# Expert blocks of a routed MoE: the next block's rows transposed behind the gate and up products, and loaded as half rows on 128 partitions

## The reference, cut to what matters

```
A = T * TOP_K_IN_GROUP                      # 512 tokens, 2 experts each
...                                         # assignments sorted by expert, rows padded to blocks
def run_block(args):
    tok, e, wt = args
    xb = h[tok]
    y = (jax.nn.silu(xb @ w_g[e]) * (xb @ w_u[e])) @ w_d[e]
    return y.astype(jnp.float32) * wt[:, None]
...
out = jnp.zeros((T, D), jnp.float32).at[row_tok].add(ys.reshape(P, D))
```

## Time and profile before

| | us |
|---|---|
| median of 3 runs (3201.56 to 3216.19) | 3206.61 |
| the profiled execution, its own time | 3209.52 |
| its span, first to last instruction | 3207.7 |

### The profile page before, as it was taken

How to read it: one execution, slowest core, us unless ns; L and a number is a source line. 1 busy time by engine, 2 the same in 40 slices (tenths; PEclk the granted TensorE clock), 3 DMA queues, 4 the chain that set the end, 5 groups by cost and what they waited for, 6 DMA issues and landing times.

```text
span 3207.7 us, 29346 instructions
## 1 busy us (share of the span) xinstructions
PE 2334.1 (73%) x9978; PEld 1037.1 (32%) x9978; DVE 1449.1 (45%) x3427; ACT 730.4 (23%) x1764; POOL 616.6 (19%) x604
## 2 busy tenths in 40 slices
PE   2998999966777778489976797655775665665554
PEld 1444554442333333145555644221221111111110
DVE  1395520140000000210127766755767777777775
ACT  2005420011000000121225544222222322232222
POOL 1001100000000000100001222234444444444442
PEclk8999999968998898788888878777878877788776
DMA  7417824818999999542105676789999999999996
GB/s 265 154 53 241 299 72 133 260 73 322 387 378 379 371 377 387 177 142 94 53 27 209 267 306 242 298 331 393 416 418 421 422 421 421 421 409 421 421 421 271
DMA packets 207405, 928.24 MB, mean 289 GB/s; under 512 B 18857, under 2 KB 58856, under 8 KB 124846
## 3 DMA queue, kind: packets, MB, share of 16 engines
q0 software_dynamic: 80752, 558.26, 43.0%
q1 hardware_dynamic: 116736, 359.68, 30.9%
q10 hardware_dynamic: 9790, 8.73, 0.8%
HBM read 891.42 MB, written 35.18 MB: 289 GB/s over the span
## 4 chain that ended last, share of the span: by engine, by line
PE 30%; DMA 25%; DVE 11%; ACT 5%; issue 5%; POOL 1%; ACTq 1%; DVEq 0%; SPq 0%; POOLq 0%
DMA ring<-in_expert_pair,ids 13%; PE bank L2026 7%; PE bank L1820 7%; DMA ring<-in_w_exp_up 6%; PE bank L2333 4%; DVE ring L1769 4%; PE bank L1826 3%; DMA pair_last<-in_expert_pair,ids 2%; PE bank L2039 2%; DMA arena_v<-in_expert_pair,ids 2%; DMA arena_h<-in_expert_pair,ids 2%; ACT arena_w L1222 1%; PE bank L2346 1%; POOL ring L845 1%; DVE pair_last L1769 1%
## 5 line engine op out<-in xcount | busy, mean ns | idle before, releaser
L2333 PE MATMUL bank<-ring,arena_w 128*32 128x512 f32 x1568 | 550.9, 821 | 359.9 <-ACT arena_w L1222 359.8
L845 POOL DMA_INDIRECT ring<-in_expert_pair,ids x392 | 424.8, 1084 | 1125.9 <-PE bank L2333 674.4
L1820 PE MATMUL bank<-arena_h,ring 128*128 128x512 f32 (+1 forms) x1024 | 372.2, 524 | 12.8 <-DMA ring<-in_w_in 10.7
L2026 PE MATMUL bank<-ring,arena_h 128*64 128x512 f32 x1056 | 288.8, 707 | 78.1 <-DMA ring<-in_w_exp_up 39.1
L2333 PEld LDWEIGHTS bank<-ring,arena_w 128*32 128x32 f32 x1568 | 94.6, 131 | 673.6 <-ACT arena_w L1222 506.7
L1769 DVE CUSTOM_DVE_ANT_0 ring<-ring,arena_h 128x1024 f32<-128x1024 f32 x203 | 245.8, 1226 | 123.1 <-DMA ring<-in_expert_pair,ids 90.0
L1769 DVE CUSTOM_DVE_ANT_0 ring<-ring 128x1024 f32<-128x1024 f32 x189 | 229.6, 1225 | 77.3 <-DMA ring<-in_expert_pair,ids 69.0
L1515 DVE TENSOR_TENSOR arena_q<-arena_q,bank 128x256 f32<-128x256 f32 x32 | 13.5, 421 | 536.9 <-ACT arena_q L1006 536.9
L1820 PEld LDWEIGHTS bank<-arena_h,ring 128*128 128x128 f32 x1024 | 178.6, 196 | 195.6 <-issue 192.6
L1220 ACT ACTIVATE arena_w<-arena_w 128x2 f32<-128x2 f32 (+1 forms) x224 | 45.6, 203 | 763.7 <-DVE arena_w L1769 763.4
L2026 PEld LDWEIGHTS bank<-ring,arena_h 128*64 128x64 f32 x1056 | 107.3, 162 | 235.0 <-issue 202.3
(11 more groups left out here) (465 smaller groups left out, 3199.4 us busy)
## 6 DMA issues: line engine op xcount, KB each, us to landing
ring<-in_w_exp_gate SPq DMA_DIRECT2D x33, 2048.0 KB, 20.2
ring<-in_w_exp_up SPq DMA_DIRECT2D x33, 2048.0 KB, 24.9
ring<-in_w_exp_down SPq DMA_DIRECT2D x33, 2048.0 KB, 25.4
ring<-in_w_in SPq DMA_DIRECT2D x15, 2048.0 KB, 22.3
ring<-in_w_mod SPq DMA_DIRECT2D x12, 2048.0 KB, 11.9
ring<-in_w_ada SPq DMA_DIRECT2D x12, 2048.0 KB, 17.7
xs_d<-zeros SPq DMA_DIRECT2D x1, 12032.0 KB, 69.3
arena_h<-xs_d SPq DMA_DIRECT2D x33, 256.0 KB, 25.6
```

The lines of the kernel that those rows point to most:

```text
L845: pool.indirect_dma_start(pair[pair_of(m)], None, A["expert_pair_2"], bass.IndirectOffsetOnAxis(ap=ids[n % 2][:, r:r + 1], axis=0)).then_i ...
L1820: mm = pe.matmul(dst, w[:, c, at], rhs[:, c, :], start=(c == 0), stop=(c == chunks - 1))
L2026: mm = pe.matmul(bank[2 + b][at, :].rearrange("p (g f) -> p g f", g=2), xbT[b][:, c, :], gu[:, :, c, 256 * half:256 * half + 256], start=( ...
L2333: mm = pe.matmul(bank[4 + 2 * (n // H % 2) + half][at, :], sel_q[:, n % 2, k0 + j, :], pair[pair_of(m + j)][:, D + 512 * half:D + 512 * ha ...
```

## The change

The rows are loaded as two half rows of 2 KB, values 0 to 511 on partitions 0 to 63 and values 512 to 1023 on partitions 64 to 127; so four transposes of 128x128 take the place of eight of 64x128. For the chunks of `xbT` to fit, partition p now takes the gate and up rows 4p to 4p+3 and 512+4p to 512+4p+3: two pieces of 8 KB. In the streams of TensorE and ScalarE the work is put in another order: transposes of e+1 between gate/up of e and down of e; the copy of e+1 ahead of e's result. The overflow block has the new layout and keeps its order.

```diff
-        xblk = [arena_h[0:CAP, D * i:D * i + D] for i in range(2)]
+        xblk = [arena_h[:, 512 * i:512 * i + 512] for i in range(2)]
...
-            return w[e, :, :].rearrange("(p c) n -> p c n", c=DC)
+            return w[e, :, :].rearrange("(h p c) n -> p h c n", h=2, c=DC // 2)
...
             def rows(e, b):
                 unless_first(sp, xbT_done, e - 1)
-                sp.dma_start(xblk[b], xs_d[bass.ds(e * CAP, CAP), :]).then_inc(xb_in[b], 16)
+                for half in range(2):
+                    sp.dma_start(xblk[b][CAP * half:CAP * half + CAP, :], xs_d[bass.ds(e * CAP, CAP), 512 * half:512 * half + 512])\
+                        .then_inc(xb_in[b], 16)
...
-                        sp.dma_start(slab(n + k), A[w][bass.ds(e, 1), :, :].rearrange("o (p c) n -> p (o c) n", c=DC))\
+                        sp.dma_start(slab2h(n + k), A[w][bass.ds(e, 1), :, :].rearrange("o (h p c) n -> p (o h) c n", h=2, c=DC // 2))\
...
-            def expert(e, b, i):
+            def columns_in(e, b):
                 act.wait_ge(xbT_done, e + 1)
                 unless_first(act, gu_done, e - 1)
-                act.activation(xbT[b], bank[b][:, :].rearrange("p (a c) -> p a c", c=CAP), ACT.Copy).then_inc(xbT_out, 1)
+                act.activation(xbT[b].rearrange("p (h c) t -> p h c t", h=2), bank[b][:, :].rearrange("p (c h t) -> p h c t", h=2, t=CAP),
+                               ACT.Copy).then_inc(xbT_out, 1)
+
+            def gate(e, b):
                 act.wait_ge(gu_done, e + 1)
...
+            def rows_out(e, b, i):
                 act.wait_ge(dn_done, e + 1)
...
+            def two(i):
+                columns_in(i * 2, 0)
+                rows_out(i * 2 - 1, 1, i - 1)
+                gate(i * 2, 0)
+                columns_in(i * 2 + 1, 1)
+                rows_out(i * 2, 0, i)
+                gate(i * 2 + 1, 1)
...
             def block_T(b):
-                for c in range(DC):
-                    mm = pe.transpose(bank[b][:, c * CAP:(c + 1) * CAP], xblk[b][:, c:D:DC], ident[0:CAP, 0:CAP])
+                for c in range(DC // 2):
+                    mm = pe.transpose(bank[b][:, c * P:(c + 1) * P], xblk[b][:, c:512:DC // 2], ident[:, :])
...
+            def columns(b, i):
+                pe.wait_ge(xb_in[b], i * 32 + 32)
+                pe.sem_inc(mark, 1)
+                block_T(b).then_inc(xbT_done, 1)
+
+            def gate_up(e, b, i):
                 pe.wait_ge(xbT_out, e + 1)
...
+            def down(e, b, i):
                 pe.wait_ge(hid_done, e + 1)
                 hidden_T(b).then_inc(hidT_pe, 1)
                 pe.wait_ge(hidT_done, e + 1)
-                arrived(2)
-                unless_first(pe, yv_done, e - 1)
-                block_dn(b, n + 2).then_inc(dn_done, 1)
+                arrived(b, i, 2)
+                unless_first(pe, yv_done, e)
+                block_dn(b, N_EXP + 3 * b + 2).then_inc(dn_done, 1)
...
+            columns(0, 0)
+            gate_up(0, 0, 0)
+            columns(1, 0)
+            down(0, 0, 0)
+            gate_up(1, 1, 0)
             with pe.Fori(1, NE // 2) as i:
-                for b in range(2):
-                    expert(i * 2 + b, b, i)
+                columns(0, i)
+                down(i * 2 - 1, 1, i - 1)
+                gate_up(i * 2, 0, i)
+                columns(1, i)
+                down(i * 2, 0, i)
+                gate_up(i * 2 + 1, 1, i)
+            down(NE - 1, 1, NE // 2 - 1)
```

More of the change, by code:

```diff
@@ L491, in build @@
         for e in range(2):
-            slabs += [(w_gu(A["w_exp_gate"], e), (DC, F), gu_done, 2 * NE), (w_gu(A["w_exp_up"], e), (DC, F), gu_done, 2 * NE),
+            slabs += [(w_gu(A["w_exp_gate"], e), (2, DC // 2, F), gu_done, 2 * NE), (w_gu(A["w_exp_up"], e), (2, DC // 2, F), gu_done, 2 * NE),
                       (w_dn(A["w_exp_down"], e), (2, 2, D), dn_done, 2 * NE)]
@@ L662, in _ @@
                     e = sp.value_load(over_i[0:1, bass.ds(i + 1, 1)], min_val=0, max_val=NE - 1)
-                    sp.dma_start(xblk[0], xs_d[bass.ds(i * CAP + NE * CAP, CAP), :]).then_inc(ov_xin, 16)
+                    for half in range(2):
+                        sp.dma_start(xblk[0][CAP * half:CAP * half + CAP, :],
+                                     xs_d[bass.ds(i * CAP + NE * CAP, CAP), 512 * half:512 * half + 512]).then_inc(ov_xin, 16)
                     for w, k in (("w_exp_gate", 0), ("w_exp_up", 1)):
-                        sp.dma_start(slab(N_EXP + k), A[w][bass.ds(e, 1), :, :].rearrange("o (p c) n -> p (o c) n", c=DC))\
+                        sp.dma_start(slab2h(N_EXP + k), A[w][bass.ds(e, 1), :, :].rearrange("o (h p c) n -> p (o h) c n", h=2, c=DC // 2))\
                             .then_inc(ov_slab, 16)
@@ L1013, in expert @@
                                   yblk[b][CAP * half:CAP * half + CAP, :]).then_inc(y_dma[b], 16)
-            for b in range(2):
-                expert(b, b, 0)
-            with act.Fori(1, NE // 2) as i:
-                for b in range(2):
-                    expert(i * 2 + b, b, i)
+            columns_in(0, 0)
+            gate(0, 0)
+            columns_in(1, 1)
+            rows_out(0, 0, 0)
+            gate(1, 1)
+            def two(i):
[5 more added lines that the diff above has]
+                gate(i * 2 + 1, 1)
+            two(1)
+            with act.Fori(2, NE // 2) as i:
+                two(i)
+            rows_out(NE - 1, 1, NE // 2 - 1)
             act.wait_ge(route_done, 2)
@@ L1024, in _ @@
                     act.wait_ge(xbT_done, i + (NE + 1))
-                    act.activation(xbT[0], bank[0][:, :].rearrange("p (a c) -> p a c", c=CAP), ACT.Copy).then_inc(xbT_out, 1)
+                    act.activation(xbT[0].rearrange("p (h c) t -> p h c t", h=2), bank[0][:, :].rearrange("p (c h t) -> p h c t", h=2, t=CAP),
+                                   ACT.Copy).then_inc(xbT_out, 1)
                     act.wait_ge(gu_done, i + (NE + 1))
@@ L2041, in block_dn, with arrived @@
                 return mm
-            def expert(e, b, i):
-                n = N_EXP + 3 * b
-                def arrived(k):
-                    pe.wait_ge(slab_in[(n + k) % RING], i * 16 + 16 * ((n + k) // RING + 1))
-                pe.wait_ge(xb_in[b], i * 16 + 16)
+            def arrived(b, i, k):
+                n = N_EXP + 3 * b + k
+                pe.wait_ge(slab_in[n % RING], i * 16 + 16 * (n // RING + 1))
+            def columns(b, i):
+                pe.wait_ge(xb_in[b], i * 32 + 32)
                 pe.sem_inc(mark, 1)
                 block_T(b).then_inc(xbT_done, 1)
+            def gate_up(e, b, i):
                 pe.wait_ge(xbT_out, e + 1)
-                arrived(0)
-                arrived(1)
-                block_gu(b, n).then_inc(gu_done, 1)
+                arrived(b, i, 0)
+                arrived(b, i, 1)
+                block_gu(b, N_EXP + 3 * b).then_inc(gu_done, 1)
+            def down(e, b, i):
                 pe.wait_ge(hid_done, e + 1)
@@ L2058, in expert @@
                 pe.wait_ge(hidT_done, e + 1)
-                arrived(2)
-                unless_first(pe, yv_done, e - 1)
-                block_dn(b, n + 2).then_inc(dn_done, 1)
+                arrived(b, i, 2)
+                unless_first(pe, yv_done, e)
+                block_dn(b, N_EXP + 3 * b + 2).then_inc(dn_done, 1)
             pe.wait_ge(route_done, 2)
             pe.wait_ge(skT_done, 5)
-            for b in range(2):
-                expert(b, b, 0)
-            with pe.Fori(1, NE // 2) as i:
-                for b in range(2):
-                    expert(i * 2 + b, b, i)
+            columns(0, 0)
[3 more added lines that the diff above has]
+            gate_up(1, 1, 0)
+            with pe.Fori(1, NE // 2) as i:
+                columns(0, i)
[5 more added lines that the diff above has]
+            down(NE - 1, 1, NE // 2 - 1)
             n_over = pe.value_load(over_i[0:1, 0:1], min_val=0, max_val=OVER)
@@ L2072, in _ @@
                 with pe.If(i < n_over):
-                    pe.wait_ge(ov_xin, i * 16 + 16)
+                    pe.wait_ge(ov_xin, i * 32 + 32)
                     pe.sem_inc(mark, 1)
```

2 lines of the change are left out of this document (added).

## The result

The changed kernel takes 3181.48 us, median of 5 runs (3168.23 to 3188.50), against 3212.97 for the kernel before, run beside it 5 times: ratio 0.990, 95% interval 0.9879 to 0.992. That is 32 us or 1.0%, twice what can be told from no change. The forecast's own narrower range, 3190 to 3215, missed it; that the wide one holds it is because it was drawn to make room for the first rival (3171), so it is luck for the mechanism that was forecast.

A forecast was written before the change was run, and what follows sets the result against it. The prediction took the slabs' DMA rate, 18.26 us a block, as the bound. Terms -3.4 + 0.9 + 3 + 1.4 (rows in 2 KB pieces) - 3.7 = -1.8 us, on the median 3206.6 about 3205; range 3168 to 3222.

The forecast's parts named there:

- the first rival: Row loads: 64-partition rows hold up other transfers' writes; an even spread gives back 33 us, about 3171; chance 0.22.
- the one on the bound: Expert blocks: slabs at 18.26 us a block are the bound; TensorE's own period of 17.6 us is shorter.
- the pieces rival: Two lagging DMA engines: more pieces cost 50 ns each, +1.0 us a block, +30, giving 3234; chance 0.16.
- the rows rival: The same as the first rival; its sign was a rate over 395 GB/s in slices 10 to 15.
- The order: TensorE and ScalarE streams: saves TensorE 2.8 us a block, which turns into waiting for up slabs; gains only at the end.
- The gain at the end, -3.4: Expert 31: gate/up starts when its up slab lands, not 3.4 us after: -3.4 us.
- The clock's +0.9: Expert 31's gate/up: slower after a longer wait, between 0 and +1.3 us, taken as +0.9.
- Rows on 128 partitions: Row loads: the 64-partition form costs 0.5 us a block; a quarter comes back, -3.7 us, range 0 to -15.
- the damage to neighbours of the outermost bound: Expert-block DMA: 2.2 us a block unassigned to any transfer, possibly harm to neighbouring transfers; -66 us as outermost end.
- Pieces: Gate and up slab loads in 8 KB pieces: between 0 and +0.21 us a block, taken as +0.1, +3 in all.
- The added wait: TensorE: down of e now stands behind transposes that wait for the rows of e+1; cost 0.
- The TensorE rival: Expert blocks: DMA rate only follows TensorE; 68 us less, capped by 16.0 us a block of DMA, about 3139; chance 0.05.

The follow-up runs named there:

- experiment 1: Kernel before with only the new order on TensorE and ScalarE; 64-partition rows, 16 KB pieces and eight transposes kept: ratio 0.9945, 3192.31 us.
- experiment 3: Kernel before with only gate and up slabs in 8 KB pieces; old order, whole rows on 64 partitions, eight transposes: ratio 1.0012, 3210.85 us.
- experiment 5: Old order, 8 KB pieces, rows as two half-row loads, both onto the same 64 partitions, eight transposes; against the kernel before: ratio 0.9994, 3214.83 us.
- experiment 6: Kernel before with odd experts' whole rows on partitions 64 to 127, even ones' on 0 to 63: ratio 1.0005, 3215.49 us.
- experiment 7: Kernel before without the row loads of experts 2 to 31 and TensorE's wait for them: ratio 1.0002, 3213.80 us.
- experiment 2: Kernel before with only the new layout: half rows on 128 partitions, 8 KB pieces, four transposes, old order: ratio 0.9916, 3183.33 us.
- experiment 11: New layout in the old order (half rows on 128 partitions, 8 KB pieces), but eight transposes of 64x128; against the kernel before: ratio 0.9995, 3206.69 us.
- experiment 9: Changed kernel with both half rows onto the same 64 partitions and eight transposes; ratio to the kernel before 0.9999, 3215.07 us.
- experiment 10: Kernel before with four transposes of 128x128 instead of eight, all DMA unchanged: ratio 0.9984, 3203.44 us.
- experiment 8: Kernel before with ScalarE's copy of the next expert's transposed rows ahead of the two store issues; TensorE order and layout old: ratio 0.9931, 3191.95 us.
- experiment 4: Kernel before with half rows on 128 partitions and four transposes; 16 KB pieces and old order kept: ratio 0.9925, 3188.83 us.

## Why the prediction came out as it did

**The step that failed** is the one on the bound: "a true saving of 2.8 us a block for an engine that isn't the bound". The kernel before had two bounds within half a microsecond of each other. Slabs came at 17.57 us a block when TensorE never held them up (experiment 1). TensorE's own chain was put at 17.6, from one pair of gate/ups. That was luck, as the next pair in the same rows, 1274.68 to 1293.41, is 18.7 us, and no slab was waited for there either; but the mean holds, 17.58 to 17.63 in experiments 3, 5, 6 and 7. It is the 18.26 that was wrong as the queue's limit. It was measured in a kernel in which the slabs' places came free by TensorE's chain, and it is longer than the pace of the kernel itself: gate/ups 2 and 31 start 772.41 and 1293.41, 17.97 us a block, because the head start of the slabs shrank in between. So a tie was read as a clear order. What should have been looked at is the list of TensorE's waits over the whole stage: 13 for the copy, 13 for the slab. Why before falls to 18.3 us a block once the early slabs are used up, slower than either bound alone, wasn't taken apart; its gate/ups behind a slab wait are longer (9.0 us for 8.3 behind the copy), and its DMA engines lag.

**Readings in the forecast that don't hold.** TensorE isn't at 9 tenths in slices 10 to 15, but at 7 and 8. That doesn't clear it as a bound, since the chain that runs through TensorE also holds its waits for ScalarE and VectorE. "Over 5 ns more" a piece wouldn't decide for the pieces rival: 20 x 0.005 x 30 is 3 us, and 16 can be told from no change. And a rate over 395 GB/s as the sign of the rows rival is not specific: the order alone gives 395 over 780 to 1240 us (experiment 1).

**How the share misled.** The forecast took "DMA share 1.01, 1.00 and 0.98" as a sign that the engines could do no more. The same share stands at 378 GB/s before, at 399 in experiment 2 (1.01), where no slab was waited for, and at 405 after (1.02):

```profile
780.00:1240.00 460.00, 352.70 (x1484) 145.27 (x1482) 22.00 (x52) 41.04 (x78) 0.00 (x0) 0.90 1.00 378
```

```profile
780.00:1240.00 460.00, 363.87 (x1474) 134.68 (x1472) 22.85 (x54) 43.23 (x82) 0.00 (x0) 0.91 1.02 405
```

A share of 1 says that packets were under way all the time, not that they could not go faster.

**The order.** Sized right for TensorE (2.8 us a block; after, the chain from gate/up to the end of down shows no gap but 0.25 and 0.70 us), wrong for the time: forecast -3.4 + 0.9, measured -18 us (experiment 1: 0.9945 of 3212). It stops there because the slabs take over at 17.57. Only part of TensorE's saving went where the forecast put it, into waiting for up slabs: that grew from 39.1 us to 71.8, by 33 us and not by 84, and the stage ended 35 us earlier and not within 5. The gain at the end, -3.4, was right in its place: gate/up of 31 no longer waits for a copy. The clock's +0.9 didn't come: that gate/up took 8.47 us after a wait of 2.85, and 8.78 before. What was missed is the overflow block: "with no slab late" failed for its down slab, whose landing its gate/up waits for by a shared semaphore: 7.47 us idle, and 2.8 us of the stage given back.

**Rows on 128 partitions.** Forecast -3.7, bounds 0 to -15, outermost -66. In the old order, without help of the transposes, it is worth nothing (experiment 11: 0.9995), since TensorE's chain is the bound there; that the forecast didn't foresee. In the new order the layout as a whole is worth 17.57 - 16.87 = 0.7 us a block by the landings (experiment 1 against after), 22 us in 32 blocks; by the ratios, 0.9945 to 0.990, it is 14 us. Both are well past "a quarter of 0.5". Whether the price of the form alone, 0.5 us a block, is enough is open: 14 us would just fit under the -15 of a full overlap, 22 wouldn't. That other transfers gain, the damage to neighbours of the outermost bound, is argued and not shown; for it speaks that after has no lag at the end of the loop and experiments 1 and 9 do. But the lag doesn't come from the 64 partitions alone, since experiments 3, 5 and 6 have them and no lag. The first rival (3171) may have had this effect and its place right. Its number came near for half the reason: it left the order out.

The Trainium skill, "DMA: Bandwidth & Descriptors", section "Rules for kernel authors", holds that transfers to the two partition halves serialize and aren't worth the trouble, and the forecast leaned the same way. On the first part the trace agrees where two half loads are alone on the queue. After, each takes 0.8 us and the second starts when the first is done, since SyncE needs 6.34 us to issue six; before, one whole load took 1.4 us:

```profile
743.20:744.00 0.80, 0.80 (x4) 0.24 (x2) 0.00 (x0) 0.55 (x1) 0.00 (x0) 0.50 0.55 164
744.00:744.20 0.20, 0.20 (x2) 0.00 (x0) 0.00 (x0) 0.00 (x0) 0.00 (x0) 0.50 0.01 0
744.20:745.00 0.80, 0.80 (x4) 0.24 (x2) 0.00 (x0) 0.00 (x0) 0.00 (x0) 0.50 0.59 164
```

On the second part the measurement decides: onto different halves (with four transposes) the kernel runs at 405 GB/s and 16.87 us a block, onto the same half (with eight) at 381 GB/s and 18.30. Whether the halves overlap in the middle of the loop, among other loads, no row shows.

**Pieces.** Forecast +3, bounds 0 and +6 (0.21 a block), rival +30. Experiment 3: -2 to +10. But there TensorE's chain was the bound, and experiment 9 is slower than experiment 1 (18.30 to 17.57 us a block, 0.9999 to 0.9945; the only differences are the 8 KB pieces of the slabs and the rows as two loads in 2 KB pieces, on the old half). That is 17 us, about half of the pieces rival's 30, in an arrangement in which the engines lag. It was not separated further, and no run has after's order and rows with 16 KB pieces.

**The added wait** for rows ahead of down: forecast 0, measured 0.4 us in all, in two waits. **The strided copy:** 0.60 us, as before. **The four transposes** were costed at 4 x 0.334 = 1.34 and took 0.75. In the old order with the new rows they are worth some 25 us, at a higher granted clock (ratio 0.9995 in experiment 11, 0.9916 in experiment 2), an effect the forecast has no term for; with the old rows 5 us, which can't be told from 0 (experiment 10). In the changed kernel that matters less, since gate/up there starts when its slab lands. But a slab's place is freed by gate/up's end, and how much of the 14 us above is of this kind stays open.

**The TensorE rival** (3139) had the right engine and took too much: it let the slabs go at 16.0 us. With its own mechanism and 17.57 for the slabs it would have been 3187, by (18.26 - 17.57) x 32 = 22 us less, or 3197 by the gate/ups' own 17.97, and experiment 1 measured 3192.

## What to carry to other kernels

When two bounds lie within a few per cent of each other, count which of them each step waited for over the whole stage, since one pair of rows or one mean picks the wrong one, and removing either alone gives nothing (experiment 7) or stops at the other (experiments 1 and 8). Before reading a null result as "this doesn't matter", ask whether the kernel was in a place where it could matter: moving the second half rows to the other 64 partitions was worth nothing in one order (experiment 5 against 11) and, together with four transposes, 1% in the other (experiment 9 against after). And look at what stands on a helper engine between the last product and the copy that releases the next one: two DMA issues of 1.13 us there cost 22 us.

## What the runs showed of the hardware that was not expected

- With all else equal, four transposes of 128x128 went with a higher granted clock than eight of 64x128: 0.93 against 0.89 over 460 us, gate/up 8.1 against 8.9 us on average (experiments 2 and 11). In the kernel with the old rows (experiment 10) the window's clock was 0.90 with four transposes, as before, but there 8 of 26 gate/ups came after a slab wait, and took 9.2 us on average against 8.4 for the 18 behind the copy. In before it was 9.0 for 13 behind a slab and 8.3 for 13 behind the copy (my means from the timelines). Nor is it the kind of transpose alone: in experiment 7, with eight in every block and a copy wait before every gate/up, they took 8.3 us on average from 773 to 970 us and 9.1 from 978 to 1185. Why it matters was not found.
- About two of the 16 DMA engines run behind the rest in some kernels (one trace of each): share 0.09 to 0.13 and 39 to 55 GB/s for 3 us and more before the last slabs land (before, experiments 9 and 10), 0.18 to 0.20 for 4 us in experiments 1 and 8. All of these have rows on 64 partitions and wait for slabs. Experiments 3, 5 and 6 have such rows, never wait for a slab from 780 to 1240 us, and show no such lag; after and experiments 2 and 11, with rows on 128, don't either. Experiment 4, rows on 128 and 16 KB pieces, ends between: 0.29 for 4 us. Which engines, and what makes them lag, stays open.
- Removing 4% of the bytes from a queue that shows a share of 1.00 didn't move the time (1.0002, 0.9986 to 1.0018): the share went to 0.92, and TensorE's chain kept its pace.
